# Two transformer blocks on one core: softmax steps reordered, a modulation turned through DRAM, and 8 KB rows for the experts' second weights

## The reference

```python
# first block
x = x + 0.5 * swiglu(rms_norm(x, ffn1_norm), ...)           # width 2816
x = x + token_mixer(rms_norm(x, mix_norm), ...)
x = x + 0.5 * swiglu(rms_norm(x, ffn2_norm), ...)
# token_mixer: y = g0*(o_a @ w_branch_a) + g1*(o_b @ w_branch_b) + g2*(o_c @ w_branch_c), then @ w_out
#   g = sigmoid(the last 3072 of the 7880 columns of h @ w_in)
#   a: dilated attention, 4 output heads, each from 3 groups;  b: 4 heads of p0 - lam * p1
#   c: 4 heads over the 64 best keys of each query, by the score of an indexer (top_k)
# second block
m = split(silu(c) @ mod_w + mod_b, 6)                         # mod_w 1024 x 6144, for c and for c_ctx
...                                                           # a convolution branch, a recurrent branch
x = x + m[2] * rmsnorm(mixed, norm1_post)
h2 = rmsnorm(x, norm2_pre) * (1 + m[4]) + m[3]
x = x + m[5] * rmsnorm(expert_choice_moe(h2), norm2_post)
# expert_choice_moe: 16 experts, 32 tokens each; hid = silu(xe @ w1[e]) * (xe @ w3[e]); ye = hid @ w2[e]
#   w1, w3: 16 x 1024 x 2048; w2: 16 x 2048 x 1024   (402 MB together)
```

## Time and profile before

| | |
|---|---|
| median of 3 runs | 2427.25 us |
| the profiled execution, its own time | 2412.69 us |
| its span, first to last instruction | 2410.8 us |
| PE / PEld busy | 1878.8 us (78%) / 1222.2 us (51%) |
| DVE / ACT / POOL busy | 845.1 (35%) / 644.3 (27%) / 266.5 us (11%) |
| DMA | 587.77 MB, 243 GB/s over the span |

### The profile page before, as it was taken

How to read it: one execution, slowest core, us unless ns; L and a number is a source line. 1 busy time by engine, 2 the same in 40 slices (tenths; PEclk the granted TensorE clock), 3 DMA queues, 4 the chain that set the end, 5 groups by cost and what they waited for, 6 DMA issues and landing times. The chain is left out here.

```text
span 2410.8 us, 36913 instructions
## 1 busy us (share of the span) xinstructions
PE 1878.8 (78%) x15507; PEld 1222.2 (51%) x15507; DVE 845.1 (35%) x1230; ACT 644.3 (27%) x1035; POOL 266.5 (11%) x329
## 2 busy tenths in 40 slices
PE   6998988868999877898788967666667666667666
PEld 6997976757888666687777852111111011011010
DVE  4654444755455565577564551000000000000001
ACT  4334444554323254343442430000000000000001
POOL 0100023420021043300550000000000000000000
PEclk9999989989999978899997979776776776766775
DMA  6654642236986410061002458999999999999997
GB/s 196 198 183 150 191 149 71 84 105 212 309 271 209 152 63 2 2 197 58 3 3 75 158 210 355 417 416 417 417 417 417 417 417 417 417 417 417 417 417 307
DMA packets 222353, 587.77 MB, mean 244 GB/s; under 512 B 11615, under 2 KB 144190, under 8 KB 189454
## 3 DMA queue, kind: packets, MB, share of 16 engines
q1 hardware_dynamic: 221144, 585.18, 64.3%
q10 hardware_dynamic: 1078, 0.70, 0.1%
HBM read 584.75 MB, written 1.09 MB: 243 GB/s over the span
## 5 line engine op out<-in xcount | busy, mean ns | idle before, releaser
L3291 PE MATMUL ps<-ex_ring,ex_xe 128*32 128x512 f32 x1536 | 284.7, 836 | 147.4 <-DMA ex_ring<-in_exp_w 147.4
L3366 DVE TENSOR_TENSOR ex_hid<-ps,ex_silu 128x512 f32<-128x512 f32 x16 | 11.1, 692 | 893.1 <-PE ps L3291 893.1
L3291 PEld LDWEIGHTS ps<-ex_ring,ex_xe 128*32 128x32 f32 x1536 | 37.2, 125 | 389.1 <-DMA ex_ring<-in_exp_w 364.5
L209 PE MATMUL ps<-xt_hi,ffn_whi 128*128 128x256 f32 x704 | 205.1, 291 | 7.3 <-DVE xt_lo L372 7.3
L3312 PE MATMUL ps<-ex_ring,ex_ht 128*32 128x512 f32 x768 | 142.3, 838 | 87.9 <-DMA ex_ring<-in_exp_w 82.4
L210 PE MATMUL ps<-xt_lo,ffn_whi 128*128 128x256 f32 x704 | 201.0, 286 | 0.0
L211 PE MATMUL ps<-xt_hi,ffn_wlo 128*128 128x256 f32 x704 | 200.7, 285 | 0.0
L181 DVE TENSOR_TENSOR ffn_wlo<-ring,ffn_whi 128x2048 fp32r<-128x2048 f32 x66 | 154.2, 2336 | 107.5 <-ACT ffn_whi L174 107.1
L174 ACT CAST ffn_whi<-ring 128x2048 fp32r<-128x2048 f32 x66 | 125.2, 1901 | 116.9 <-PE ps L211 102.6
L209 PEld LDWEIGHTS ps<-xt_hi,ffn_whi 128*128 128x128 f32 x704 | 136.5, 194 | 17.2 <-issue 17.0
L210 PEld LDWEIGHTS ps<-xt_lo,ffn_whi 128*128 128x128 f32 x704 | 136.5, 194 | 1.2 <-issue 1.2
(11 more groups left out here) (760 smaller groups left out, 4120.1 us busy)
## 6 DMA issues: line engine op xcount, KB each, us to landing
ex_ring<-in_exp_w SPq DMA_DIRECT2D x288, 1024.0 KB, 23.4
ring<-in_exp_w SPq DMA_DIRECT2D x96, 1024.0 KB, 24.6
ring<-in_w_in SPq DMA_DIRECT2D x55, 1024.0 KB, 5.3
ring<-in_ffn_w_gate SPq DMA_DIRECT2D x22, 1024.0 KB, 6.0
ring<-in_ffn_w_up SPq DMA_DIRECT2D x22, 1024.0 KB, 5.4
ring<-in_ffn_w_down SPq DMA_DIRECT2D x22, 1024.0 KB, 4.9
ffn_mod_tile<-in_mod_w SPq DMA_DIRECT2D x12, 1024.0 KB, 6.1
xn<-in_mod_w SPq DMA_DIRECT2D x12, 1024.0 KB, 6.6
```

Source lines behind the costliest of these rows:

```text
L209: nc.tensor.matmul(out, lhs[0], rhs[0], start=start, stop=False, skip_group_check=shared)
L3291: mm = mm_(ps[32 * q:32 * q + 32, 4 + u, :], xe[:, k], expert_slot(g, n)[:, 512 * q:512 * q + 512], start=k == 0, stop=k == KC - 1)
L3366: v.tensor_tensor(hid[:], ps[:, 5, :], silu[:], ALU.mult).then_inc(S["hid"], 1)
```

## The change

It does four things. In the softmax stage, ACT copies the turned probabilities of the step before ahead of both casts of the gates; and branch c's two steps stand between a and b, for which the ranking runs two rounds per step in the first eight steps. In the second feed-forward, the partial sums of the modulation are no longer turned by PE a tile at a time: SP stores them to DRAM two steps later (two DMAs of four rows of 1 KB per tile), loads them all back with the row index on partitions, and four products in step m = 2 turn and add them; `dve_end` moves there too, and the double steps and the order of the first loads change. For the experts, a tile of w2 is one row of 8 KB per partition (two neighbouring rows of the matrix), and the columns of `hid` are turned in the order that fits.

```diff
--- softmax_units
-        steps = [(u, h0 + h, t) for u in "ab" for h0 in (0, 2) for t in range(TT) for h in range(2)] + [("c", 0, t) for t in range(TT)]
+        steps = [(u, h0 + h, t) for u in "ab" for h0 in (0, 2) for t in range(TT) for h in range(2)]
+        steps[8:8] = [("c", 0, t) for t in range(TT)]
...
                 if i:
+                    copy_turned(i - 1)
                     gates.hi(act, 12 + 2 * i)
                 if i % 2 == 0:
                     gates.copy_out(act, 2 + i // 2)
                 if i:
                     gates.hi(act, 13 + 2 * i)
-                    copy_turned(i - 1)
...
+            n_ranked = TT * rounds // 2
...
                 if i:
                     weights(i - 1)
-                rank_keys(i)
+                if i < n_ranked:
+                    rank_keys(2 * i)
+                    rank_keys(2 * i + 1)
--- ffn_phase
-                        side.dve_down(dve, k - 2 * pairs)
+                        side.dve_down(dve, ch, k - 2 * pairs)
...
-                    if side and k == 2 * pairs - 2:
-                        side.dve_end(dve, ch)
--- Modulation
-    steps = {k: 2 if k in (2, 5, 8, 11, 14) else 1 for k in range(2, 21)}
+    steps = {k: 2 if k in (5, 8, 11, 14, 17) else 1 for k in range(2, 21)}
...
+        self.sums_dram = g.post_dram[1:25].rearrange("a j d -> (a j d)").rearrange("(j r n) -> j r n", j=4, r=2)
...
+        self.sums = self.inorm[0:96].rearrange("r (j p) -> r j p", j=4)
...
-        sp.dma_start(self.sel[:], I["k_modsel"]).then_inc(S["sel"], 16)
+        self.load_tile(sp, 0)
         for dst, src in ((self.feat[:], I["k_feat"]), (self.w1[:], ...
             sp.dma_start(dst, src).then_inc(S["ffn_in"], 16)
+        sp.wait_ge(S["squares"], TT)
+        self.load_tile(sp, 1)
         for dst, src in ((self.fz[:], ...), (self.decay[:], ...)):
             sp.dma_start(dst, src).then_inc(S["hy_consts"], 16)
-        self.load_tile(sp, 0)
-        sp.wait_ge(S["squares"], TT)
-        self.load_tile(sp, 1)
...
+    def store_sums(self, sp, i):
+        sp.wait_ge(self.S["mod_rows"], i + 1)
+        for r in range(2):
+            sp.dma_start(self.sums_dram[:, r, 256 * i:256 * i + 256], self.rows[r:97 + r:32, i % 2, :]
+                         ).then_inc(self.S[f"mod_stored{i % 2}"], 16)
+
+    def load_sums(self, sp):
+        S = self.S
+        for i in range(2):
+            sp.wait_ge(S[f"mod_stored{i}"], 16 * self.n_tiles)
+        sp.wait_ge(S["spectrum"], 5)
+        for r in range(2):
+            sp.dma_start(self.sums[48 * r:48 * r + 48], self.sums_dram[:, r, :].rearrange("j (m p) -> m j p", p=P)
+                         ).then_inc(S["mod_back"], 16)
+
     def load(self, sp, k):
+        for i in range(self.n_tiles):
+            if self.step_of[i] == k - 2:
+                self.store_sums(sp, i)
         for i in range(2, self.n_tiles):
             if self.step_of[i - 2] == k - 1:
...
     def pe(self, pe, k):
-        for i in self.of.get(k - 1, ()):
-            pe.wait_ge(S["mod_rows"], i + 1)
-            for s in range(2):
-                m = 2 * i + s
-                mm = mm_(ps[:, 6, 2 * m:2 * m + 2], self.rows[:, i % 2, P * s:P * s + P], self.sel[:], start=True, stop=True)
-            mm.then_inc(S["mod_turned"], 1)
...
     def load_context(self, sp):
+        for i in range(self.n_tiles):
+            if self.step_of[i] > 2 * FC // 2 - 3:
+                self.store_sums(sp, i)
+        self.load_sums(sp)
         sp.wait_ge(self.S["mod_used"], self.n_tiles)
...
     def pe_down(self, pe, m, hid, n_hid):
+        if m == 2:
+            pe.wait_ge(hid, n_hid)
+            pe.wait_ge(self.S["mod_back"], 32)
+            for j in range(4):
+                mm = self.nc.tensor.matmul(self.ps[:, 0, 0:96], self.sums[:, j, :], self.g.ident[0:96, 0:96], start=j == 0, stop=j == 3)
+            mm.then_inc(self.S["mod_turned"], 1)
...
-    def dve_down(self, dve, m):
+    def dve_down(self, dve, ch, m):
+        if m == 2:
+            self.dve_end(dve, ch)
...
     def act(self, act, k):
             act.wait_ge(S["mod_used"], i + 1)
             if i >= 2:
-                act.wait_ge(S["mod_turned"], i - 1)
+                act.wait_ge(S[f"mod_stored{i % 2}"], 32 * (i // 2))
--- load_expert_tile
-        src = I["exp_w2_2"][0].rearrange("e (h k p) n -> p k (e h) n", h=2, p=P)[:, j % KC, bass.ds(2 * e, 2), :]
-        dst = slot.rearrange("p (h n) -> p h n", h=2)
+        src = I["exp_w2_2"][0].rearrange("e (k p h) n -> p (e k) (h n)", h=2, p=P)[:, bass.ds(KC * e + j % KC, 1), :]
+        dst = slot.unsqueeze(1)
--- expert_phase
-                    mm = nc.tensor.transpose(ps[:, 6, P * c:P * c + P], hid[:, P * c:P * c + P], g.ident[:])
+                    cols = hid[:].rearrange("s (k p h) -> s k h p", k=2, h=2)[:, c // 2, c % 2, :]
+                    mm = nc.tensor.transpose(ps[:, 6, P * c:P * c + P], cols, g.ident[:])
...
-                            q, f = 2 * n + h, 2 * h + k // 4
-                            mm = mm_(ps[32 * q:32 * q + 32, 7, :], ht[:, k % 4, CAP * f:CAP * f + CAP], w[:, h, 512 * n:512 * n + 512],
+                            q, f = 2 * n + h, k // 2
+                            mm = mm_(ps[32 * q:32 * q + 32, 7, :], ht[:, 2 * (k % 2) + h, CAP * f:CAP * f + CAP], w[:, h, 512 * n:512 * n + 512],
```

More of the change, by code:

```diff
@@ L1240, in rank_keys @@
                 t, r = i // rounds, i % rounds
-                if t >= TT:
-                    return
                 nk, b0 = causal_keys(t)
@@ L1251, in rank_keys @@
                     ch(v.tensor_scalar(keep[:, t, 0:nk], sel[:, 0, 0:nk], -1.0, -MASKED, ALU.add, ALU.mult))
-            assert TT * rounds <= steps.index(("c", 0, 0))
+            n_ranked = TT * rounds // 2
+            assert n_ranked <= steps.index(("c", 0, 0))
             for i in range(len(steps)):
@@ L1690, in __init__ @@
         self.n_tiles = n
-        self.csil, self.rows, self.sel = sb("csil", [P, KC, 32]), sb("mod_rows", [P, 2, 256]), sb("mod_sel", [P, 2])
+        self.csil, self.rows = sb("csil", [P, KC, 32]), sb("mod_rows", [P, 2, 256])
+        self.sums_dram = g.post_dram[1:25].rearrange("a j d -> (a j d)").rearrange("(j r n) -> j r n", j=4, r=2)
         self.post, self.slot = sb("post", [P, 2, KC]), sb("mod_tile", [P, WT])
@@ L1794, in pe_read @@
     def pe_read(self, pe):
-        pe.wait_ge(self.S["mod_read"], 1)
+        pe.wait_ge(self.S["mod_rows"], self.n_tiles)
+        pe.wait_ge(self.S["spectrum"], 5)
     def load_context(self, sp):
+        for i in range(self.n_tiles):
+            if self.step_of[i] > 2 * FC // 2 - 3:
+                self.store_sums(sp, i)
+        self.load_sums(sp)
         sp.wait_ge(self.S["mod_used"], self.n_tiles)
@@ L1806, in pe_down @@
             pe.wait_ge(self.S["normed"], m - 3)
+            pe.wait_ge(self.S["mod_read"], 1)
             for q in (2 * m - 8, 2 * m - 7):
@@ L1921, in dve_end @@
         S, g, v = self.S, self.g, self.nc.vector
-        dve.wait_ge(S["mod_turned"], self.n_tiles)
+        dve.wait_ge(S["mod_turned"], 1)
         m3 = g.mod[:].rearrange("p (m r) -> p m r", r=2)
-        v.tensor_tensor(m3, self.ps[:, 6, 0:96].rearrange("p (m r) -> p m r", r=2),
+        v.tensor_tensor(m3, self.ps[:, 0, 0:96].rearrange("p (r m) -> p m r", r=2),
                         col(g, "mod_b_2", 0, 48).unsqueeze(2).to_broadcast([P, 48, 2]), ALU.add).then_inc(S["mod_read"], 1)
```

1 line of the change is left out of this document (removed).

## The result

The changed kernel takes 2390.77 us in the median of 4 runs (2384.77 to 2401.42), the kernel before, measured beside it, 2424.24 us: ratio 0.9868, 95% interval 0.982 to 0.9916, or 33.5 us faster. Run again later with 6 runs it took 2389.09 us against 2416.26: ratio 0.9879, interval 0.9854 to 0.9904, 27.2 us. The profiled execution took 2395.82 us with a span of 2394.0, only 16.9 us under the span before; where the difference between 33.5 and 16.9 lies is part of what follows.

A forecast was written before the change was run, and what follows sets the result against it. Transfers alone were taken to bound the experts, a chain of waits the softmax stage, PE the second feed-forward. Terms -9.0, -18.0 and -16.0 sum to -43.0 us, from 2427.25 to 2384 us, range 2373 to 2402.

The forecast's parts named there:

- Experts, -9.0: Expert stage: w2's tiles in rows of 8 KB move at w1's 421 GB/s instead of 409, saving 9.0 us.
- Softmax, -18: Softmax stage: 26.0 us of waits and half clock removed, 7.6 given back, so 18 us saved.
- the 2.4 us of waits in b's eight steps: Softmax stage, branch b: waits for DVE given back, 0.3 us for each of eight steps.
- those of 0.6, 0.7 and 1.0: Softmax stage, given back: 0.6 us for doubled first ranking rounds, 0.7 for c's second step, 1.0 for the casts.
- Second feed-forward, -16: Second feed-forward: 18.7 us removed, 1.5 of added products and 1.3 of added waits given back, so 16 us saved.
- 96 weight loads of 191 ns that stand alone in PE's queue, 12.3 us: Second feed-forward: dropping PE's turning of the sums a tile at a time removes these loads, saving 12.3 us.
- the wait for the third tile: Second feed-forward, early steps: PE's 4.76 us wait goes because step 2 uses one modulation tile instead of two.
- the 1.6 us put for the clock: Second feed-forward: about half of 3.4 us lost to a clock of 0.83 over 20 us, counted as removed.
- the modulation's tiles come late: Rival, second feed-forward: shorter steps ask for more DMA and the wait moves; gain there 5 us, 2395 us, chance 0.12.
- The stores: Second feed-forward: ACT's copies wait for stores of sums to DRAM, but these land before its next cast; cost nothing.
- the slower case: Rival, second feed-forward: stores landing after about 13 us hold ACT's copy and the cast behind it; 2434 us, chance 0.03.
- The added products, 1.5: Second feed-forward, step m = 2: four added products of 96 columns cost PE 1.5 us with the wait around them.

The follow-up runs named there:

- late_doubles: The changed kernel with the modulation's double steps at 8, 12, 14, 17 and 20 instead of 5, 8, 11, 14 and 17: 2385.07 us, run again 2376.43 us.
- rows_only: The kernel before with w2 in rows of 8 KB alone: 2405.82 us, ratio 0.9962.

## Why the prediction was right, and where its terms were not

The forecast was 2384 us with a range of 2373 to 2402; 2390.77 and 2389.09 lie in it. Against the 43 us of the sum, the medians have 33.5 and 27.2, and the stages of the trace 30.8. Of the three terms two were right, and the third, the second feed-forward's, was three times too large.

- **Experts, -9.0: right.** -8.9 and -9.3 in the two profiles of the changed kernel, -9.2 alone. No 409 level is left. The estimate by the Trainium skill ("DMA: Bandwidth & Descriptors", section "Why small descriptors are slow (HBM only)"), 3.6 us for a cost of about 3 cycles per packet, is not borne out: 3 of the 131 cycles of a 4 KB row would be 3.7 of its 160 ns, and the three row sizes give 9 ns.
- **Softmax, -18: right within about a microsecond (-16.8).** The waits for the copy went; the sign "under 10 us ahead of the turning" is 7.7. The longest wait was forecast at 2.9 us, at the place where the ranking's end stands ahead of c's logits, and it is 3.79:

```profile
437.48 0.95 PE L1100 MATMUL ps<-ident,logits 128*128 128x128 f32 x6 [3.79 <-DVE rden L1209]
```

  VectorE shows the chain that it waits for (start, length). The ranking's last round begins at 428.03, its end runs to 433.82, c's logits to 437, and the weights come last:

```profile
428.03 0.43 DVE L990 MAX8 top<-proj 128x8 f32<-128x256 f32 x1
428.49 0.35 DVE L1002 TENSOR_SCALAR proj<-proj,top 128x256 f32<-128x256 f32 x1
...
429.53 1.14 DVE L1005 TENSOR_SCALAR proj<-proj,top 128x256 f32<-128x256 f32 x1
...
433.82 0.76 DVE L1184 SCALAR_TENSOR_TENSOR logits<-ps,bias 128x256 f32<-128x256 f32 x2
434.61 1.62 DVE L1193 TENSOR_TENSOR logits<-logits,keep 128x512 f32<-128x512 f32 x1
436.26 0.69 DVE L1198 TENSOR_REDUCE stats<-logits 128x4 f32<-128x512 f32 x1
...
437.27 0.15 DVE L1209 RECIPROCAL rden<-stats 128x1 f32<-128x1 f32 x1
```

  The stage was forecast at about 99 us, it is 100. Of its smaller terms, the 2.4 us of waits in b's eight steps are 3.9 us in five; those of 0.6, 0.7 and 1.0 have no row of their own.
- **Second feed-forward, -16: wrong, it is -5.1, and -3.4 in the second profile.** Two terms failed. The first: "96 weight loads of 191 ns that stand alone in PE's queue, 12.3 us" are worth 7.4 us. The 12.3 are the time in which these loads were busy, 0.51 us per tile. On PE's path they take 0.44 per tile, and 0.16 us of that comes back in every step. The lengths of the steps, which I didn't take, show the first of these already before: those of k = 8 and k = 9 differ by one turned tile and are 8.71 and 8.27 us. By that the term would have been 10.6; what comes back no row before shows. The second: the wait for the third tile (4.76 us) went, as forecast, and 1.3 us was put for those that come back. They are 6.9. The kernel before had 6.6, since a second wait of 1.9 us is not in the sum. So the waits gained nothing where the sum had 3.5. With products at half clock behind two of the waits (16 products in 1.71 and 1.94 us, 1.07 elsewhere), the 1.6 us put for the clock didn't come either:

```profile
597.28 1.07 PE L1772 MATMUL ps<-xn,ffn_csil 128*32 128x256 f32 x16
601.70 1.71 PE L1772 MATMUL ps<-ffn_mod_tile,ffn_csil 128*32 128x256 f32 x16 [3.35 <-DMA ffn_mod_tile<-in_mod_w]
...
660.26 1.94 PE L1772 MATMUL ps<-xn,ffn_csil 128*32 128x256 f32 x16 [2.42 <-DMA xn<-in_mod_w]
```

  I had step 5's second tile come in time, because I counted one tile's landing per step and not what stands ahead of its issue. SyncE shows it. PE wants the tile at 598.35. Its slot is free at 590.8, but it is issued at 592.81, behind the ring's load at 591.33, which waited for its own slot, and behind the store of the sums at 591.74. It lands 8.9 us later, with the queues at a share of 1.10, where the forecast had 6.6:

```profile
584.05 1.69 SPq L1732 DMA_DIRECT2D gated_post_norms<-ffn_mod_rows  x2
585.78 0.95 SPq L1726 DMA_DIRECT2D xn<-in_mod_w  x1
591.33 0.37 SPq L145 DMA_DIRECT2D ring<-in_ffn_w_up  x1
591.74 1.02 SPq L1732 DMA_DIRECT2D gated_post_norms<-ffn_mod_rows  x2
592.81 0.44 SPq L1726 DMA_DIRECT2D ffn_mod_tile<-in_mod_w  x1
```

  That was the mechanism of the rival "the modulation's tiles come late" (chance 0.12). Its gain of 5 us for the stage came out too, but in part by accident: lateness and its clock make up about six of the 11 us that are missing, the price of the loads the other five. late_doubles confirms the lateness, since the same bytes asked later give 7 us. Two of the prediction's signs say so by themselves: it was to be wrong if PE waits for `mod_w` in more than two places, and it waits in three; and PE was to run without a wait near 605 us, where one of 3.35 ends at 601.7.
- **The stores: cost put at nothing, and by way of ScalarE it is nothing on PE.** But the sign "the copies of the sums not waited for behind stores" is wrong. ScalarE waited in 9 of its 24 copies, 5.9 us at the longest:

```profile
ACT ffn_mod_rows L1883 <- DMA gated_post_norms<-ffn_mod_rows: 15.6, 9, 5.9
```

  ScalarE was idle behind PE before too, and no wait of PE in that stage names it; so the slower case has its mechanism in the trace and not its price. The transfers into and out of that DRAM tensor land after 3.8 us in the median and 5.3 at most, in line with the 5 us that the prediction had worked out from the Trainium skill's 2 us ("DMA: Bandwidth & Descriptors", section "Anatomy of one DMA — SWDGE (gpsimd) path"), and far from the 13 of the slower case:

```profile
DMA to landing us min/median/max: 2.1/3.8/5.3
```

  What wasn't priced is SyncE's time: a pair of stores holds its queue for 1.0 us in 18 of 24 cases and for up to 2.8 us, in front of the tile's load. Of the 2.0 us by which the tile above is issued late, 1.0 is such a pair.
- **The added products, 1.5: 1.0**, and `mod_back` isn't waited for. Eight passes from 751.7 to 752.6:

```profile
L1828 PEld LDWEIGHTS ps<-ident,ffn_inorm x8: 188/192/193, 751.7 to 752.6; 96*128 96x128 f32 x8
L1828 PE MATMUL ps<-ident,ffn_inorm x8: 247/276/276, 752.0 to 752.7; 96*128 96x96 f32 x8
```

- **The clock.** The prediction took the stages beside the change as constant. Of the 14 us between the 30.8 of the changed stages and the 16.9 of the two spans, 11.4 are the half clock in the chunk steps. Anyone who had compared two spans would have put it on the change; whether the change has a part in how often it comes is open.

So the forecast of the time was good in part by luck. Its range was wide enough for a term that was 11 us too large, and it started from 2427.25 us, the highest median of the kernel before. In the sets measured later that kernel has 2424.24, 2416.26, 2413.48, 2417.91 and 2420.85. From the 2416.26 that stand beside the changed kernel's 2389.09, the same 43 us would have given 2373, which is 16 us too low. (The range's lower end is also 2 us off its own terms, which give 2371 us.)

## What to carry to other kernels

Price removed short products by how the length of a step changes, not by their busy time, and expect less from removing than adding costs: a pass with a load of 191 ns cost 0.11 us when added and gave 0.07 when removed. When transfers are the near limit, a prefetch into one free slot has to be counted from its issue in the queue, with all that stands ahead of it, and it pays to put the double loads where the queues have room. Before a difference of two spans is put down to a change, compare the starts of the same instructions stage by stage: an untouched stage had taken two thirds of what a whole part brought.

## What the runs showed of the hardware

- Rows of 2, 4 and 8 KB ran at 387, 409 and 421 GB/s; one fixed cost of about 9 ns per row and DMA engine fits all three.
- The same stage of one program ran at 0.50 of the clock for 30.7 us in one execution, and at full clock but for 3.4 us in another; in the 28.3 us before it PE had been busy for 22.1 us in the one and 21.8 in the other, at full clock. The 12 runs of that program lie in two groups whose middles are about 12 us apart.
- One of the 12 executions of rows_only took 4662.38 us, for which nothing here has an explanation; without it the median is 2405.58 instead of 2405.82.
- The kernel with late double steps is the fastest that the runs bear out without useless work: 2385.07 and 2376.43 us (ratios 0.9859 and 0.9835) against 2390.77 and 2389.09 (0.9868 and 0.9879) of the changed kernel. The intervals overlap, so its 7 us rest on the stage in the trace and on medians that point the same way.
